# The opening of a two-layer encoder kernel: order of weight splits, squares of x and stores

## The reference, cut to what matters

```python
h = rmsnorm(x, g_mix[i])                        # needs mean(x * x) per token
mem_kv = rmsnorm(mem, g_mem[i]) @ w_mem_kv[i]    # 1024 x 1024 weights, both layers
kh = rmsnorm(k, g_k[i])                          # per head of 128
scores = qh @ kh * 128 ** -0.5                   # then softmax, @ vh
```

## Time and profile before

| | us |
|---|---|
| median of 3 runs | 2619.14 (2618.55 to 2621.78) |
| profiled execution | 2626.81 |
| its span | 2625.1 |
| TensorE busy in the span | 2547.0 (97%) |
| VectorE, ScalarE, GpSimd busy | 1804.9, 1210.2, 745.7 |

### The profile page before, as it was taken

The page is one execution under the profiler, slowest core; times in us unless marked ns, Lnnn a source line. Parts: engine busy times, 40 slices in busy tenths (PEclk is TensorE's granted clock), DMA queues, the critical chain, the costliest instruction groups (busy, mean ns, idle before and its releaser), DMA issues.

```text
span 2625.1 us, 34703 instructions
## 1 busy us (share of the span) xinstructions
PE 2547.0 (97%) x12264; PEld 2124.9 (81%) x12264; DVE 1804.9 (69%) x2243; ACT 1210.2 (46%) x2029; POOL 745.7 (28%) x537
## 2 busy tenths in 40 slices
PE   8899999999999999999999999997899999999999
PEld 7788887888888887887878888886788888887887
DVE  6576666167756667775678888887648765758667
ACT  6572333144434443335666666665323443434322
POOL 2513220102323223233024444443121322222322
PEclk9999999999999999999999999999899999999999
DMA  5411225213433446544111111112321352437634
GB/s 209 161 49 57 88 81 200 79 58 117 145 119 120 151 166 259 220 149 158 43 45 34 33 32 32 33 32 107 144 89 57 132 168 72 156 132 275 244 142 157
DMA packets 85922, 311.39 MB, mean 119 GB/s; under 512 B 10416, under 2 KB 10416, under 8 KB 73136
## 3 DMA queue, kind: packets, MB, share of 16 engines
q1 hardware_dynamic: 74304, 261.17, 28.1%
q0 software_dynamic: 11216, 42.47, 4.6%
q10 hardware_dynamic: 288, 6.29, 0.6%
HBM read 220.24 MB, written 89.65 MB: 118 GB/s over the span
## 4 chain that ended last, share of the span: by engine, by line
PE 82%; DVE 7%; issue 5%; DMA 2%; ACT 2%; POOL 1%; SPq 1%; DVEq 0%; ACTq 0%; POOLq 0%
PE ps L2361 25%; PE ps L2363 25%; PE ps L2362 25%; PE ps L2673 2%; DVE keep L1920 1%; PE ps L2622 1%; PE ps L2689 1%; PE ps L2690 1%; PE ps L2623 1%; DMA tile_lo<-d_tile 1%; POOL sig L973 1%; DVE tile_lo L2230 1%; DVE sk_lo L1950 1%; DVE w_lo L1602 1%; PE ps L2491 0%
## 5 line engine op out<-in xcount | busy, mean ns | idle before, releaser
L2361 PE MATMUL ps<-tile_hi,g_hi 128*128 128x512 f32 x1680 | 660.5, 393 | 7.7 <-DVE tile_lo L2230 5.2
L2363 PE MATMUL ps<-tile_hi,g_lo 128*128 128x512 f32 x1680 | 657.5, 391 | 0.0
L2362 PE MATMUL ps<-tile_lo,g_hi 128*128 128x512 f32 x1680 | 654.2, 389 | 0.0
L2361 PE MATMUL ps<-xg_hi,w_hi 128*128 128x512 f32 x1024 | 406.0, 396 | 4.5 <-DVE xg_lo L1790 3.3
L2363 PE MATMUL ps<-xg_hi,w_lo 128*128 128x512 f32 x1024 | 402.1, 393 | 0.0
L2362 PE MATMUL ps<-xg_lo,w_hi 128*128 128x512 f32 x1024 | 401.6, 392 | 0.0
L2361 PEld LDWEIGHTS ps<-tile_hi,g_hi 128*128 128x128 f32 x1680 | 315.8, 188 | 76.2 <-issue 6.1
L2363 PEld LDWEIGHTS ps<-tile_hi,g_lo 128*128 128x128 f32 x1680 | 315.7, 188 | 71.2
L2362 PEld LDWEIGHTS ps<-tile_lo,g_hi 128*128 128x128 f32 x1680 | 315.8, 188 | 68.7
L1500 ACT ACTIVATE g_hi<-quads 128x512 fp32r<-128x512 f32 x310 | 194.9, 629 | 355.9 <-PE ps L2363 326.5
L2159 DVE TENSOR_TENSOR g_lo<-quads,g_hi 128x512 fp32r<-128x512 f32 x310 | 283.5, 915 | 103.1 <-ACT g_hi L1500 99.0
(11 more groups left out here) (270 smaller groups left out, 4303.9 us busy)
## 6 DMA issues: line engine op xcount, KB each, us to landing
quads<-wpack SPq DMA_DIRECT2D x62, 1024.0 KB, 6.1
raw<-wpack SPq DMA_DIRECT2D x88, 512.0 KB, 3.2
d_split<-x SPq DMA_DIRECT2D x116, 256.0 KB, 6.3
tile_lo<-d_tile SPq DMA_DIRECT2D x30, 512.0 KB, 7.2
d_tile<-R SPq DMA_DIRECT2D x46, 256.0 KB, 6.4
d_tile<-x SPq DMA_DIRECT2D x46, 256.0 KB, 6.2
cquads<-wpack SPq DMA_DIRECT2D x10, 1024.0 KB, 4.9
tile_hi<-d_split SPq DMA_DIRECT2D x10, 1024.0 KB, 8.3
```

What stands on the lines that cost most here:

```text
L2361: pe.matmul(out, whi, mhi, start=start, stop=False, skip_group_check=chained)
L2362: pe.matmul(out, whi, mlo, start=False, stop=False, skip_group_check=chained)
L2363: return pe.matmul(out, wlo, mhi, start=False, stop=stop, skip_group_check=chained)
```

## The change

In stage A of layer 1 the splits of blocks 14 and 15 move, on ScalarE and VectorE, to the two sides of the normed keys of layer 0. The squares of x leave the loop over n: row block 0 comes behind the first value copies of layer 1, row blocks 1 and 2 at the end of stage A, 3 to 7 in stage B behind the splits of blocks 18 and 19 and ahead of the scaling of x, which now waits for them. GpSimd adds all eight row blocks ahead of layer 1's stores and none ahead of layer 0's, and waits for all stores once, at the end. TensorE begins block 8 without a wait for layer 0's value copies.

```diff
--- before.py
+++ after.py
@@ -869,8 +869,9 @@
                         pool.tensor_copy(R[:, ln[h]], squares[nu][:, h, :]).then_inc(acc_added, 1)
 
             for i in range(LAYERS):
-                for m in range(MHEADS * i, MHEADS * (i + 1)):
-                    add_squares(0, m)
+                if i == LAYERS - 1:
+                    for m in range(KB):
+                        add_squares(0, m)
 
                 pool.wait_ge(ka_lo_ready, i + 1)
                 pool.wait_ge(evacuated, base["A", i][2] + A_UNITS)
@@ -878,7 +879,7 @@
                     pool.dma_start(d_kv[i, n], t[:]).then_inc(kv_stored, 16)
                 for n, t in enumerate((va_hi, va_lo)):
                     pool.dma_start(d_kv[i, 2 + n], t[:].rearrange("p a c -> p (a c)")).then_inc(kv_stored, 16)
-                pool.wait_ge(kv_stored, 64 * (i + 1))
+            pool.wait_ge(kv_stored, 64 * LAYERS)
 
             for i in range(LAYERS):
                 if i > 0:
@@ -1123,28 +1124,32 @@
                     if i > 0:
                         for h in range(2):
                             split(0, MHEADS + n, h)
-                        square(0, n)
                 if i > 0:
+                    prep(u0 + MHEADS + 2)
                     key_hi(i - 1)
+                    prep(u0 + MHEADS + 3)
                 act.wait_ge(evacuated, v0 + MHEADS)
                 act.activation(ksq[:], kf[:], ACT.Square).then_inc(ksq_ready, 1)
                 for g in range(2):
                     for n in (2 * g, 2 * g + 1):
-                        prep(u0 + MHEADS + n + 2)
+                        if i == 0 or g > 0:
+                            prep(u0 + MHEADS + n + 2)
                         if i == 0:
                             for h in range(2):
                                 split(0, n, h)
-                        else:
-                            square(0, MHEADS + n)
                     act.wait_ge(w_used, u0 + MHEADS + 2 * g + 2)
                     if i > 0:
                         act.wait_ge(kv_stored, 64 * i)
                     for mb in range(2):
                         act.activation(va_hi[:, mb, g * 2 * P:(g + 1) * 2 * P], ps[:, value_bank(i, g) + mb, 0:2 * P],
                                        ACT.Copy, scale=mcol[:, mb:mb + 1]).then_inc(va_hi_ready, 1)
+                    if i > 0 and g == 0:
+                        square(0, 0)
                 act.wait_ge(kstat_full, i + 1)
                 act.activation(root[:], ps[:, value_bank(i, 0), 0:KB], ACT.Sqrt, bias=eps[:, 0:1]
                                ).then_inc(kroot_ready, 1)
+            for m in range(1, 3):
+                square(0, m)
 
             for i in range(LAYERS):
 
@@ -1159,6 +1164,8 @@
                 if i == 0:
                     prep(u0 + 2)
                     prep(u0 + 3)
+                    for m in range(3, KB):
+                        square(0, m)
 
                 def query_half(h, half):
 
@@ -1192,6 +1199,7 @@
 
                 if i == 0:
                     act.wait_ge(xg_lo_ready, 2 * KB)
+                    act.wait_ge(sq_ready, 2 * KB)
                     for m in range(KB):
                         act.activation(x[:, m, :], x[:, m, :], ACT.Copy, scale=gain[:, 0, 0, m:m + 1]
                                        ).then_inc(x_scaled, 1)
@@ -2419,7 +2430,7 @@
             for i in range(LAYERS):
                 u0, f0, v0 = base["A", i]
                 if i > 0:
-                    pe.wait_ge(evacuated, v0)
+                    pe.wait_ge(evacuated, v0 - MHEADS)
                 for n in range(MHEADS):
                     if i > 0 or n > 0:
                         memory_keys(i, n)
```

## The result

The changed kernel is slower. Ten runs of each gave 2630.41 us (median, 2627.56 to 2632.89) after and 2622.41 us (2618.55 to 2628.13) before: a ratio of 1.0027, 95% interval 1.0017 to 1.0037, which is +7.1 us with 4.5 to 9.7 around it. I had forecast 2623.6 us with "within 0.2%" as the likeliest case and a range up to 2629; the median lies 1.4 us above the range. The three runs of before that the forecast started from (2619.14) lay low: in later batches the same kernel had medians of 2624.86, 2625.13, 2624.16 and 2624.07 us (35, 24, 23 and 17 runs). The later batches ran on four different chips, each with the kernel before beside it, so kernels are compared by their ratio to it.

What follows compares the result with a forecast made beforehand. TensorE, busy 97% of the span, was taken as the bound. The front wins 8.9 us, the back needs 13.4 more: +4.5 us, from a median of 2619.1 to 2623.6 us, range 2616 to 2629.

Steps and rivals of the forecast that it cites:

- The front: Opening up to block 16 used up: both TensorE gaps go, block 14 follows without a stall; gain 8.9 us.
- rival (c): In front: VectorE's slow splits are not GpSimd's doing, front wins about 5 us; sum +8, 2627; chance 0.07.
- the cold restart: TensorE at block 16 after two short rests: 1.5 us charged for half clock, ends 0 and 2.8.
- U: The moment block 16 is used up: forecast at 90.0 us, against 98.9 before.
- The back: From U to the first scores, through squares, adds, stores, copies and loads: 30.6 us, 13.4 more than before.
- TensorE's query statistics, 1.8 us: Behind the query copies, ahead of the twelve matmuls: statistics priced at 1.8 us.
- The twelve matmuls: 512-column matmuls between query statistics and first scores: 4.2 us taken, between 2.7 warm and 5.2 cold.
- have no price of their own, since they end before the loads: In the back: norm statistics and the two shorter TensorE waits add nothing to the sum.
- the rule against the change: Idle gaps throttle TensorE, each restart is paid; waits in the back and ahead of block 16 cold: +5.8, 2624.9.
- (a): Gain is kept because GpSimd's chain behind U is shorter than TensorE's 17.2 us: -7 us, 2612; chance 0.15.
- (b): The back costs more: GpSimd's in-order queue, slower adds push stores, query copies and loads: +7, 2626.2; chance 0.11.

Runs made afterwards that it cites:

- e4: The changed kernel with 16 and 34 spare 512-column matmuls keeping TensorE busy through both waits: +2.9 us against before, 4.2 better than after.
- e12: The kernel before, unchanged, profiled again: no time of its own given; scores at 119.3 to 120.2 us over this and e13.
- e13: The kernel before, unchanged, profiled once more after e12: no time of its own given; scores at 119.3 to 120.2 us over both.
- e7: The changed kernel with squares 1 to 7 earlier, stores behind five adds, x scaled behind the first query copies: 5.2 us below before.
- e3: The changed kernel with layer 1's stores issued behind three row blocks of adds, the other five behind them: +4.7 us against before.
- e1: The kernel before with the new front alone (no TensorE wait at block 8, blocks 14 and 15 split around the normed keys): +2.6 us.
- e9: The kernel before with only the splits of blocks 14 and 15 moved around the normed keys, TensorE's wait kept: +2.9 us.
- e6: The changed kernel with layer 1's key statistics in their own bank and blocks 16 and 17 split ahead of the value copies: 4.7 us below before.
- e8: The changed kernel with the edits of e6 and e7 together: 10.2 us below before.
- e11: The kernel of e8 with the first two squares made in ScalarE's rest ahead of layer 1's value copies: 12.6 us below before.
- e5: The kernel of e1 with GpSimd's wait for the stores taken to the end: 4.7 us below e1, a little below before.
- e10: The kernel before with only GpSimd's wait for the stores taken to the end: nothing done to the time.
- e14: The kernel before with six spare 512-column matmuls between the norm and query statistics: +1.0 us, interval holds 0.
- e2: The changed kernel with all squares at the end of the keys' stage, undoing the late squares alone: 2623.14 us, level with before.

## Why the prediction was wrong

**The front came as forecast.** No gap at 45 us, block 14 right behind block 13, x pairs at 1.41 and weight splits at 1.23 us (rival (c) has fallen), stores of layer 0 issued at 62.55 (62.8) and released at 71.51 (71.4), block 16 at 75.69 (75.6). One term was small: the cold restart. From block 16's start to U took 15.2 us against 12.9 before, 2.3 instead of the 1.5 charged. U is 90.9 instead of 90.0.

**The back has the forecast's chain, in its order, with four terms too small.** Behind U the query copies start at 22.9 us instead of 22.1 (adds 13.0 against 12.6; stores 8.4 against 7.4, inside the 7.4 to 9.8 that I gave; ScalarE goes on 0.3 us before GpSimd does, so not all of it shows here). The copies take 2.1 (2.0). Then the step that failed most: "TensorE's query statistics, 1.8 us", which I took from a warm row. They stand behind a wait of 6.5 us, and the next matmul starts 3.4 us after the first of them (115.95 to 119.39). The twelve matmuls take 5.3 where I took 4.2, between 2.7 warm and 5.2 cold. The sum is 33.8 against 30.6, and with U the scores are at 124.7 instead of 120.6: 4.1 us, of which 0.9 is U (0.8 of it the restart), 0.8 the adds and stores, 0.1 the copies, 1.6 the statistics and 1.1 the matmuls, less 0.5 because TensorE and not the load is last. Of the 4.1 us some 3.5 are half clock, and they were in my own text: I foresaw the 8 us of emptiness ahead of the statistics and still gave them the warm price. The sentence "have no price of their own, since they end before the loads" is wrong for the wait that ends last: its cold restart lay on the path. e4 took 2.0 us of it back and then met the load, 31.1 us behind its U, where my sum had 30.6.

My own working of the rule against the change was wrong too. I let it turn 1.5 us into 2.8 and got +5.8 with the loads last. Worked through, cold statistics (3.4, after) and cold matmuls (5.2) end at U + 24.1 + 3.4 + 5.2 = 32.7, behind the loads at 30.6; with U at 91.3 the scores come at 124.0, +7.9, against the measured 124.66. The Trainium skill (TensorE: Matmul & The Clock Gate, "HAM oscillation"), by which idle gaps throttle the array and the restart is paid again at each, agrees with this trace for all three long gaps: 4.31, 3.56 and 8.9 us at 0.50 stand behind them.

**The other side of the difference was off too.** The two traces differ by 8.6 us at the scores, but the 116.08 of before belongs to an execution in which the clock held through the two rows of statistics. e12 and e13 show the unchanged kernel at 119.3 and 120.2, so the usual shift is 4.5 to 5.4 us, and behind the attention +5.0. My +4.5 was therefore near the typical shift, by luck: two errors of about 4 us cancel in it, a back priced too warm and a baseline that was too warm. In time the shift is +7.1, with 4.5 as the low end of its interval. Between about 5 in the traces and 7.1 in the runs 2 us stay open; the table's two columns differ by as much for kernels in which nothing else changed. The absolute miss of 6.8 us is 3.3 us of starting point (2622.41 against the 2619.14 that I added to) and 3.5 us of difference (8.0 between the medians, against 4.5).

**The rivals.** (a), gain kept, fell: TensorE waits 3.9 and 6.5 us in the back. It needs both the stores and the scaling of x out of the way of the query copies, as in e7. (b) is not what happened, though its time (2626.2) is nearer: adds at a pitch of 1.30 us are below the 1.33 from which it was to decide. With the one more us of the stores its mechanism brings 0.8 us to the query copies and 1.1 us to the loads, a part of the miss and the smaller one. Its condition, the in-order GpSimd queue, is right in kind, and e3 shows that it is half the story: with the stores in front the scaling of x, in order on ScalarE, arrives 1.2 us earlier than the stores did.

**What I had not seen.** The front's gain hangs on the rest of the change. e1 and e9 show that the moved splits without the moved squares cost 2.6 and 2.9 us (both intervals down to about 0), since the buffers of the squares tie ScalarE to GpSimd and GpSimd to the stores. And the gain could have been kept: e6 leaves the back as it is and only lets TensorE run through in front (-4.7 us), e7 takes the last squares out of the way of the stores and of the query copies (-5.2), and e8 and e11 do both (-10.2 and -12.6).

## What to carry to other kernels

Price a moved step by what stands behind it in each in-order queue until the next point where the chains meet: here ten adds, four stores and one scaling, which gave back all of an 8 us gain in front. A matmul behind a wait of several us gets its half-clock price, and if that wait ends last the price lies on the path. Before a difference of a few us is read from two profiles, take one of the unchanged kernel a second time: its clock alone moved the same mark by 4 us.

## What the runs showed of the hardware

- TensorE's clock fell to 0.50 without any gap in its busy time. It happened behind two rows of sixteen one-column matmuls, and once, in e12, behind a single such row (TensorE was busy for 1.91 of the 2.00 us from 84 us on). With no gap ahead of the two rows it was so in seven of nine executions (e1, e5, e9, e10, e11, e12, e13); it held in the first profile of before and in e7. From the first of the twelve matmuls of 512 columns behind them to the scores it then takes 4.3 (e5) to 5.3 us (e10, e12, e13), by how early the fall comes, instead of 2.9 (the first profile of before). That the one-column matmuls are the cause is a reading of these runs and of the one profile of e14; it isn't shown. e10, where nothing on this path was changed, shows the fall step by step (windows):

```profile
109.92:111.62 1.70, 1.70 (x18) 1.70 (x16) 1.15 (x3) 1.70 (x5) 0.71 (x2) 1.00 1.05 347
111.62:114.00 2.38, 2.38 (x18) 2.38 (x18) 1.64 (x4) 1.08 (x3) 0.00 (x0) 0.74 1.02 346
114.00:116.00 2.00, 2.00 (x6) 1.61 (x7) 1.36 (x7) 1.59 (x3) 0.18 (x1) 0.50 0.88 322
```

- Four stores of 512 KB from GpSimd took 7.4, 8.4 (after) and 11.9 us (e2) from first issue to release. Weight loads beside them are a part of it, not all: two ran beside the 11.9 and also beside the 9.8 of before, none beside the 8.4.
- A row of sixteen one-column matmuls takes 1.84 us at full and 3.55 us at half clock: even work with almost no columns pays the clock in full.
